# An attention phase that shares one ring of PSUM banks: who copies which half of the attention values, and where value transposes stand

## The reference

```python
proj = h @ w_in                       # q, k, v of three groups, and a gate
for g, (window, dil) in enumerate(((128, 1), (512, 4), (2048, 16))):
    scores = einsum(qs, kb) / 8 + alibi           # keys of a window, by stride dil
    m = max(scores); p = exp(scores - m); z = sum(p)
    o = einsum(p, vb) / z; lse = m + log(z)
    ...
wts = softmax(stack(lses))            # over the three groups, per head and row
o = sum over g of wts[g] * outs[g]
y = (o * silu(gate)) @ w_out
```

## Time and profile before

| | |
|---|---|
| median of three runs | 2034.8 us (2034.26 to 2035.8) |
| the profiled execution | 2039.31 us, span 2037.4 us |
| TensorE busy | 1951.9 us, 96% of the span |
| VectorE busy | 1336.6 us, 66% |
| ScalarE busy | 1057.7 us, 52% |
| GpSimd busy | 1271.5 us, 62% |
| share of TensorE in the chain that ended last | 70% |
| granted TensorE clock, mean | 0.993 |

### The profile page before, as it was taken

How to read it: one execution, slowest core, us unless ns; L and a number is a source line. 1 busy time by engine, 2 the same in 40 slices (tenths; PEclk the granted TensorE clock), 3 DMA queues, 4 the chain that set the end, 5 groups by cost and what they waited for, 6 DMA issues and landing times.

```text
span 2037.4 us, 34018 instructions
## 1 busy us (share of the span) xinstructions
PE 1951.9 (96%) x12487; PEld 1543.8 (76%) x12487; DVE 1336.6 (66%) x2659; ACT 1057.7 (52%) x2586; POOL 1271.5 (62%) x841
## 2 busy tenths in 40 slices
PE   7999999999999999999999999899999999999998
PEld 4777777777777777777777877688778778777887
DVE  7547556476565564655657776698598498487553
ACT  5454554555545445455455255575575575575320
POOL 0566775857758668677576355376476476586572
PEclk8999999999999999999999999999999999999999
DMA  9111221222212222122125433565365355376431
GB/s 303 43 58 58 76 93 55 80 68 76 83 55 77 91 55 78 58 76 84 55 85 198 152 119 55 144 186 145 127 183 151 122 179 150 124 195 229 176 124 42
DMA packets 117605, 229.50 MB, mean 113 GB/s; under 512 B 22465, under 2 KB 55873, under 8 KB 117441
## 3 DMA queue, kind: packets, MB, share of 16 engines
q1 hardware_dynamic: 117440, 227.32, 36.3%
HBM read 199.42 MB, written 27.86 MB: 112 GB/s over the span
## 4 chain that ended last, share of the span: by engine, by line
PE 70%; DVE 13%; issue 5%; ACT 3%; DMA 3%; POOL 3%; SPq 3%; DVEq 0%; ACTq 0%; POOLq 0%
PE pp L699 25%; PE pp_s L2592 15%; PE po L699 8%; PE tp L776 3%; PE po L852 2%; PE sp_ L766 2%; DVE stage_s L3272 2%; PE pp_s L2796 2%; PE yo_p L2796 2%; DVE spare L1561 2%; PE st_p L2609 2%; PE st_p L2796 1%; PE fill L2796 1%; DVE vv L3193 1%; PE yo_p L2624 1%
## 5 line engine op out<-in xcount | busy, mean ns | idle before, releaser
L699 PE MATMUL pp<-h_forms_hi,w_f 128*128 128x512 f32 x1576 | 517.5, 397 | 1.5 <-POOL w_f L584 1.5
L699 PEld LDWEIGHTS pp<-h_forms_hi,w_f 128*128 128x128 f32 x1576 | 298.0, 189 | 64.9 <-POOL w_f L584 4.2
L699 PE MATMUL pp<-h_forms_lo,w_f 128*128 128x512 f32 x788 | 308.5, 391 | 0.0
L584 POOL TENSOR_TENSOR w_f<-w_raw,w_f 128x512 fp32r<-128x512 f32 x154 | 199.2, 1312 | 157.4 <-ACT w_f L1059 157.2
L2592 PE MATMUL pp_s<-h_hi,w_hi_s 128*128 128x512 f32 x624 | 269.6, 432 | 5.3 <-DVE stage_s L3272 2.7
L1120 ACT ACTIVATE prob<-prob,mz 128x256 f32<-128x256 f32 (+2 forms) x384 | 170.0, 444 | 196.0 <-DVE mz L1403 195.3
L2592 PE MATMUL pp_s<-h_hi,w_lo_s 128*128 128x512 f32 x624 | 244.9, 392 | 0.0
L2592 PE MATMUL pp_s<-h_lo,w_hi_s 128*128 128x512 f32 x624 | 244.1, 391 | 0.0
L699 PE MATMUL po<-h_forms_hi,w_f 128*128 128x512 f32 x632 | 208.3, 390 | 0.0
L584 POOL TENSOR_TENSOR w_f<-w_f_raw,w_f 128x512 fp32r<-128x512 f32 x117 | 152.3, 1301 | 88.2 <-ACT w_f L1059 85.2
L699 PEld LDWEIGHTS pp<-h_forms_lo,w_f 128*128 128x128 f32 x788 | 149.3, 190 | 28.7
(11 more groups left out here) (572 smaller groups left out, 4489.3 us busy)
## 6 DMA issues: line engine op xcount, KB each, us to landing
w_raw<-in_a_w SPq DMA_DIRECT2D x80, 512.0 KB, 3.3
rw<-cum_rows SPq DMA_DIRECT2D x32, 1024.0 KB, 5.9
w_raw_s<-in_b_w SPq DMA_DIRECT2D x40, 512.0 KB, 4.3
ew<-exp_rows SPq DMA_DIRECT2D x64, 256.0 KB, 7.0
v<-in_ada_w SPq DMA_DIRECT2D x48, 256.0 KB, 3.3
qk<-merge_rows SPq DMA_DIRECT2D x42, 256.0 KB, 4.3
yT_b<-trunk SPq DMA_DIRECT2D x32, 256.0 KB, 2.6
stage_s<-yT_b SPq DMA_DIRECT2D x14, 512.0 KB, 5.0
```

What stands on the lines that cost most here:

```text
L584: return nc.gpsimd.tensor_tensor(out, x, hi.bitcast(F32), ALU.subtract)
L699: last = nc.tensor.matmul(bank, w[:, b], h[:, b], start=b == 0 and t == 0, stop=b == KS - 1 and t == 2)
```

## The change

ScalarE now copies the second half of the values, which stands in the ring `tp`, and does it at once; VectorE adds the first half from `op` later in the step, behind the copies of the probabilities and `tops`. "x" is no longer an event of the table: the second half goes to the bank of the last event of its duo. Three semaphores take the place of `first_half_in` and of the table's "x": `x_full` (values done), `x_out` (ScalarE's copy done), `x_joined` (VectorE's addition done). The second "p" group of a step waits for `x_out`, the next values wait for `x_joined`.

The transposes of value tiles (steps 0, 3, 8) and of the statistics (step 9) move behind the first product of the half unit; in the last pair's step 3 they stand behind the third product, and its step 8 keeps its order. In odd steps ScalarE's `numerators` goes ahead of rounding 5. VectorE adds `sum_of_third` right behind the sum ahead of it. Two semaphores of the second layer are reused ones with another start value, since three new ones are needed.

The core of the diff:

```diff
             for d in range(DUOS):
-                if d:
-                    out += [("x", d - 1)]
-                v_events = [("v", V_AT[d], 0), ("v", V_AT[d], 1)] if d in V_AT else []
-                p_events = [("p", 2 * d), ("p", 2 * d + 1)]
-                out += p_events + v_events if d == 8 and early else v_events + p_events
+                out += [("p", 2 * d), ("p", 2 * d + 1)]
+                if d in V_AT:
+                    out += [("v", V_AT[d], 0), ("v", V_AT[d], 1)]
...
+        def last_event(table, d):
+            return table[("v", V_AT[d], 1)] if d in V_AT else table[("p", 2 * d + 1)]
+
+        def second_bank(table, d):
+            return (last_event(table, d) + 2) % 2 if d < DUOS - 1 else table[("p", 2 * d + 1)] % 2
...
                     product(n, 0, b0)
+                    if after_first:
+                        after_first()
...
                 def transpose_probs(j, u, at, par):
                     pe.wait_ge(p_ready, UNITS * j + (u + 1))
                     pe.wait_ge(t_free, T0 + at + 1)
+                    if u % 2 and (j or u > 1):
+                        pe.wait_ge(x_out, DUOS * j + u // 2)
...
-                    pe.wait_ge(t_free, T0 + at + 2)
+                    pe.wait_ge(t_free, T0 + at + 3)
                     if j or d:
-                        pe.wait_ge(first_half_in, DUOS * j + d)
+                        pe.wait_ge(x_joined, DUOS * j + d)
...
-                        if d == DUOS - 1:
-                            new_stats(j, T_AT)
-                            second_half(n)
-                        elif d % 2:
-                            second_half(n)
+
+                        def other_transposes():
+                            new_v(j, d, T_AT)
+                            if d == DUOS - 1:
+                                new_stats(j, T_AT)
+
+                        if d % 2:
+                            second_half(n, other_transposes)
                         else:
-                            first_half(n)
+                            first_half(n, other_transposes)
...
                 def numerators(j, d):
-                    act.wait_ge(t_full, T0 + NT * j + (T_LAST if j == PAIRS - 1 else T_AT)[("x", d)] + 1)
+                    act.wait_ge(x_full, DUOS * j + d + 1)
+                    src = tp[:, second_bank(T_LAST if j == PAIRS - 1 else T_AT, d), 0:2 * P]
...
                 def odd_step(j, n, kinds, numerators_of, softmax_of):
+                    numerators_of()
                     round_form(n, 5)
-                    numerators_of()
                     round_form(n, 6)
...
-                def join_values(j, d, table):
+                def join_values(j, d):
-                    src = tp[:, n % 2, 0:2 * P]
-                    dve.wait_ge(t_full, T0 + NT * j + n + 1)
+                    src = op[:, 0:2 * P]
+                    dve.wait_ge(x_out, DUOS * j + d + 1)
...
+                def duo(ch, j, d, beside=None):
                     if beside:
                         beside()
-                    event(j, ("p", 2 * d), table)
-                    event(j, ("p", 2 * d + 1), table)
+                    event(j, ("p", 2 * d), T_AT)
+                    event(j, ("p", 2 * d + 1), T_AT)
                     if d < DUOS - 1:
                         tops(j, 2 * d + 2)
                         tops(j, 2 * d + 3)
+                    joined(j, d)
+                    new_v(j, d, T_AT)
+                    if d == 9:
+                        event(j, ("s", 0), T_AT)
```

More of the change, by code:

```diff
@@ L321, in t_events @@
                 if d == 9:
-                    x = ("x", DUOS - 1)
-                    out += [("s", 0), x, ("s", 1)] if early else [("s", 0), ("s", 1), x]
+                    out += [("s", 0), ("s", 1)]
             return out
@@ L732, in fourth_product, with second_half @@
                     product(n, 3, b0)
-                def second_half(n, between=None):
+                def second_half(n, after_first=None, between=None):
                     pe.wait_ge(w_ready, FORMS * n + 5)
@@ L1299, in _ @@
                 a, b, c = LAST_UNITS
+                numerators(j, 0)
                 round_form(a, 5)
-                numerators(j, 0)
                 round_form(a, 6)
@@ L1336, in _ @@
                 round_form(c, 4)
+                numerators(j, 6)
                 round_form(c, 5)
-                numerators(j, 6)
                 round_form(c, 6)
@@ L1676, in _, with joined, new_v @@
                 second_sums(1)
-                def duo(ch, j, d, table, last_pair, beside=None, third=None):
+                def joined(j, d):
                     if d:
-                        join_values(j, d - 1, table)
+                        join_values(j, d - 1)
                     elif j:
-                        join_values(j - 1, DUOS - 1, T_AT)
-                    if third is not None:
-                        sum_of_third(third)
+                        join_values(j - 1, DUOS - 1)
+                def new_v(j, d, table):
                     if d in V_AT:
@@ L1714, in next_rows @@
                         weigh_next(j, NEXT_AT[d])
-                duo(ch0, 0, 0, T_AT, False)
+                duo(ch0, 0, 0)
                 first_sums(FIRST_UNITS)
@@ L1724, in _ @@
                             gate_columns()
-                        duo(ch, j, d, T_AT, False, None, n if d % 2 else None)
+                        duo(ch, j, d)
                         if d == 8:
@@ L1734, in _ @@
                             second_sums(n, lambda: next_rows(j, d))
-                    duo(ch, j + 1, 0, T_AT, False, lambda: shares(ch, j))
+                    duo(ch, j + 1, 0, lambda: shares(ch, j))
                     first_sums(5 * j + (FIRST_UNITS + 5))
@@ L1748, in _, with third, sixth @@
                 a, b, c = LAST_UNITS
-                def at(d):
-                    return lambda: duo(ch, j, d, T_LAST, True)
-                def at_six():
-                    duo(ch, j, 6, T_LAST, True)
+                def third():
+                    last_duo(j, 3)
+                    new_v(j, 3, T_LAST)
+                def sixth():
+                    last_duo(j, 6)
                     weigh_next(j, (0, 1, 2))
-                duo(ch, j, 1, T_LAST, True, None, a)
+                last_duo(j, 1)
                 second_sums(a)
-                duo(ch, j, 2, T_LAST, True)
-                first_sums(b, at(3))
-                duo(ch, j, 4, T_LAST, True, None, b)
-                second_sums(b, before_last=at(5))
-                first_sums(c, at_six)
-                duo(ch, j, 7, T_LAST, True, None, c)
-                second_sums(c, lambda: y_rest(0))
-                join_values(j, 7, T_LAST)
-                event(j, ("p", 16), T_LAST)
-                event(j, ("p", 17), T_LAST)
-                tops(j, 18)
-                tops(j, 19)
-                for half in range(2):
-                    event(j, ("v", 2, half), T_LAST)
+                last_duo(j, 2)
+                first_sums(b, third)
+                last_duo(j, 4)
+                second_sums(b, before_last=lambda: last_duo(j, 5))
+                first_sums(c, sixth)
+                last_duo(j, 7)
+                second_sums(c, lambda: y_rest(0))
+                last_duo(j, 8)
+                new_v(j, 8, T_LAST)
                 event(j, ("e", 0), T_LAST)
-                duo(ch, j, 9, T_LAST, True)
+                last_duo(j, 9)
+                event(j, ("s", 0), T_LAST)
                 y_rest(1)
                 weigh_next(j, (3, 4, 5))
-                join_values(j, DUOS - 1, T_LAST)
+                join_values(j, DUOS - 1)
                 silu(j, PP_FREE_END - 3, 0)
```

90 lines of the change are left out of this document (44 added, 46 removed).

## The result

The changed kernel takes 1998.8 us (1997.0 to 1999.9, four runs) against 2035.3 of the kernel before: a ratio of 0.982 with an interval of 0.980 to 0.984, 36.5 us saved. The prediction had 2013 with a range of 2004 to 2033. The direction was right and the time lies outside the range: the gain is 14.7 us larger than the sum of 21.8. The profiled execution took 1997.65 us with a span of 1995.8.

The account below looks back on a forecast made before the run. TensorE's waits for VectorE, some 38 us in all, were taken as the recoverable time. Gains and losses by place summed to 21.8 us, which off the median of 2034.8 gives 2013, range 2004 to 2033.

Parts of the forecast that it names:

- Step 6: Values of duo 5: the second transposes no longer wait for VectorE's addition; 2.12 us in each of seven pairs, 14.8 us gained.
- GpSimd's give-back: Product after the duo 5 step: GpSimd's low part has only 1.43 us of room; 0.2 us lost per pair, 1.4 in all.
- Step 3: Value transposes move inside the stream of products and a wait goes; 0.85 us in each of seven pairs, 6.0 us gained.
- Step 8: ScalarE's copy stays late behind the gate, yet the second product starts earlier; 1.07 us in each of seven pairs, 7.5 gained.
- Steps 9 and 0: Pair boundary: later statistics delay the chain through HBM and ScalarE's copy; 1.3 us at each of seven, 9.1 us lost.
- four of the seven late ones: Pair boundaries where the differences begin 7.4 to 8.6 us behind the statistics' copy; some 2.3 us lost at a late one.
- estimate of 4 us for two transfers in a row: Statistics' store and load, by the Trainium skill: boundaries would cost nothing and the gain be near 31 us.
- The clock: TensorE's half clock behind idles: 3.4 us goes with the removed wait, one new fall comes at late boundaries; net 1.7 gained.
- (a): Rival: GpSimd's chain keeps its old times and becomes the pace; price 9.4 us, time 2023; chance 0.15 together with (d).
- (d): Rival: ScalarE's copies come as late as VectorE's addition did; some 2025; chance 0.15 together with (a).
- (b): Rival, pair boundary: all loads land late, half clock follows each idle; 4.6 us left, 2030 or no change; chance 0.10.
- (c): Rival, pair boundary: the chain through HBM becomes the bound; 5.4 us each, 37.8 in all, 2040, slower; chance 0.12.

Follow-up runs that it names:

- the copy ahead of the gate: Changed kernel with ScalarE's copy of duo 7's second bank ahead of the gate's last two evacuations; 1992.0 us, ratio 0.979.
- the statistics ahead: Changed kernel with the statistics' transpose put back ahead of the first product of a pair's last step; 2006.3 us, ratio 0.986.
- the exchange alone: Changed kernel with transposes of values and statistics back ahead of the product, the swapped banks kept; 2009.9 us, then 2006.7 us in a second try with corrected order.
- GpSimd behind the shares: Changed kernel with GpSimd's first difference of weights in a pair's first step waiting until VectorE has finished the shares; 1998.8 us.
- delayed stores: Changed kernel with each store of group 0's statistics cut in two, so that the load follows four issues later; 2010.1 us, ratio 0.987.
- the copy ahead of the exponential: Changed kernel with ScalarE's copy of duo 9's second bank ahead of its exponential for the shares; 1999.3 us, ratio 0.982.

## Why the prediction was wrong

*Step 6* (14.8): 15.2 by the lengths before and after, once the 3.1 us of half clock are taken out. Right. *GpSimd's give-back* (1.4): 1.0 in step 7, by the mechanism named. *Step 3* (6.0): 6.5. *Step 8* (7.5): 8.5, with the idle forecast. The idle's cause is shown by the copy ahead of the gate.

*Steps 9 and 0* (a loss of 9.1, 7.6 with the GpSimd waits of that place that the sum counted apart): a gain of 1.1. This is the step that failed, by 8.7 us. For an early pair it was nearly right: the second product was to lose 0.2 to 0.3 us (0.16 by the times that the prediction works out) and gained 0.05, counted from the values of step 9. The failure is "four of the seven late ones", at 2.3 each. Four late landings in one execution were taken for a property of the pairs. The fourth and fifth came from a stalled issue in SyncE, which the repeated run does not show in those places; the sixth is late in every profile with the statistics ahead and in none with them behind, so it went with the change, for a reason that no run shows. Only the last is late in every profile, and it alone was late after the change. The price was off too: late boundaries had already cost 0.6 to 1.3 us before (step 0 of 15.8 to 16.5 against 15.26), which the sum did not set against the new loss, and the one late pair of after lost 0.3 in steps 9 and 0 together, not 2.3. The run with the statistics ahead shows that the later chain, beside the moved value transposes, is no loss: in the changed kernel the shares begin ahead of GpSimd's first difference instead of beside it, and with the earlier chain they are stretched and TensorE waits for what stands behind them. Against the exchange alone it is no gain either (195.3 against 195.1 us in steps 9 and 0). The prediction's estimate of 4 us for two transfers in a row did not come: from the copy to the differences it took 6.7 us at the least.

*Not in the sum*: steps 4 and 5, 0.2 us each in every pair, 2.7 in all. The run of the exchange alone has them too; which part of the edit they come from was not tried.

*The clock* (1.7): 3.1 gone in the profiled run, and no fall in the pairs after. That was luck in both: the repeat of before had none either, and the runs with the copy ahead of the gate and with GpSimd behind the shares had a fall at the last boundary, behind idles of 2.9 and 2.7 us, where the changed kernel had 2.4.

By the profiled executions, which lie 41.7 us apart, the gain is 19.9 above the sum. Of that the boundary, steps 4 and 5, the clock, and steps 3 and 8 make 8.7 + 2.7 + 1.4 + 1.5 = 14.3; step 6, step 7 and the last pair add 1.6. Another 3.9 stand ahead of the first values and behind the last ones, where executions of the kernels above differ by as much without an edit there. How much of the 14.7 between the medians each part has is not shown, since the clock and the landings differ between executions. Of the rivals, GpSimd's pace (a) got its 0.15 us a pair and no more (by its own price its time would be 2022.4, not 2023), and (d) is excluded by step 6, which has no idle left. That the boundary gives the gain back (b) and the loss there (c) did not come, but the run with delayed stores shows their mechanism alive: 1.6 us per boundary, with half clock behind four of seven idles.

## What to carry to other kernels

A duration or a lateness that shows up in some repeats of a loop and not in others is first to be compared with a second execution, before it is counted per repeat. A wait that is to be removed in a queue is worth what the next waiter in it leaves: one copy moved ahead of the gate gave its whole idle, one ahead of the exponential gave nothing until the shares moved as well (the shares' move by itself was not tried). And where small VectorE operations lie beside GpSimd's, the chain may be shorter when it begins at another time: here the shares take 1.8 us or 5.3.

## What the runs showed of the hardware

A VectorE operation on two SBUF inputs that takes 0.21 us alone took 1.30 when it began beside a GpSimd operation of 1.29 us, and the five on the shares took 1.78 us undisturbed and up to 5.3 beside GpSimd's. Half clock followed some of TensorE's idles and not others of the same length: two of seven at 2.16 us in one run of before and none of seven in the next, two of three at 1.9 with the copy ahead of the exponential, both at 2.4 with the statistics ahead, none at the one of 2.4 in the changed kernel, four of seven at 2.5 to 2.7 with delayed stores. The Trainium skill (TensorE: Matmul & The Clock Gate, section HAM oscillation) lets only longer gaps do this; the windows at 0.83 above, behind idles of 2.5 to 2.7 us, say otherwise.
